# Turning the rows of x with a diagonal of their roots, with g_mix applied per partition

## What is computed

```
y  = x * rsqrt(mean(x * x, axis=-1) + EPS)
xn = y * g_mix
z  = xn @ w_in
```

## Time and profile before

| what | value |
|---|---|
| median of 3 runs | 1081.69 us (1081.29 to 1082.82) |
| the profiled execution's own time | 1082.38 us |
| its span, first to last instruction | 1080.6 us |
| busy over the span | TensorE 90%, weight loads 80%, VectorE 62%, ScalarE 51%, GpSimd 26% |
| bytes moved | 193.67 MB, 179 GB/s over the span |
| chain that ended last, by engine | TensorE 72%, VectorE 14%, issue 7%, ScalarE 4%, DMA 2% |

### The profile page before, as it was taken

One profiled execution on the slowest core, in us unless ns is written; L12 is line 12 of the kernel. 1 busy time (PEld: TensorE's weight loads), 2 busy tenths in 40 slices (PEclk: granted clock), 3 DMA queues, 4 the chain that ended last, 5 costly groups with the idle time before them and its releaser, 6 DMA issues.

```text
span 1080.6 us, 16629 instructions
## 1 busy us (share of the span) xinstructions
PE 975.7 (90%) x5991; PEld 861.5 (80%) x5991; DVE 671.3 (62%) x805; ACT 547.4 (51%) x605; POOL 281.4 (26%) x187
## 2 busy tenths in 40 slices
PE   3989899999999978889999999948899999999960
PEld 2989789888988976789999996837788888888750
DVE  5495659747865972621111211369999898989827
ACT  5544525714542570343333233347787878787722
POOL 2443204313330430433434345000111111101012
PEclk9999999999999998899999999968999999999995
DMA  9352122302222220123232339318999999999835
GB/s 309 125 164 59 47 67 60 94 28 87 62 59 68 58 58 20 40 62 95 79 96 78 97 123 290 149 59 293 399 409 415 413 414 413 414 413 414 314 119 206
DMA packets 146738, 193.67 MB, mean 179 GB/s; under 512 B 14486, under 2 KB 91692, under 8 KB 146576
## 3 DMA queue, kind: packets, MB, share of 16 engines
q1 hardware_dynamic: 139000, 165.27, 43.8%
q0 software_dynamic: 4656, 16.21, 3.9%
q10 hardware_dynamic: 3048, 11.75, 2.8%
HBM read 173.43 MB, written 19.77 MB: 179 GB/s over the span
## 4 chain that ended last, share of the span: by engine, by line
PE 72%; DVE 14%; issue 7%; ACT 4%; DMA 2%; DVEq 1%; POOL 0%; POOLq 0%; ACTq 0%; SPq 0%
PE PJ L447 58%; DVE MEM L1641 2%; DVE MEM_R L1847 2%; PE MS L1293 2%; PE NM L1273 2%; PE PJ L1222 1%; PE MS L1255 1%; PE MS L1456 1%; PE NM L447 1%; PE MS L1300 1%; PE MS L1268 1%; DMA MEM<-in_x_prompt_dram 1%; PE NM L1404 1%; PE MS L1283 1%; DMA MEM<-expert_rows,MEM 1%
## 5 line engine op out<-in xcount | busy, mean ns | idle before, releaser
L447 PE MATMUL PJ<-MEM_R 128*128 128x272 f32 (+2 forms) x5016 | 809.3, 322 | 18.6 <-ACT MEM L857 6.0
L447 PEld LDWEIGHTS PJ<-MEM_R 128*128 128x128 f32 x5016 | 727.8, 192 | 81.3 <-issue 10.3
L661 POOL TENSOR_TENSOR MEM_R<-RAW,MEM_R 128x1024 fp32r<-128x1024 f32 x81 | 201.6, 2498 | 371.1 <-ACT MEM_R L798 371.0
L1847 DVE TENSOR_TENSOR MEM_R<-CHUNK,MEM_R 128x2048 fp32r<-128x2048 f32 x100 | 224.6, 2285 | 16.1 <-ACT MEM_R L1056 14.8
L1056 ACT CAST MEM_R<-CHUNK 128x2048 fp32r<-128x2048 f32 x100 | 189.3, 1912 | 14.3 <-PE PJ L447 10.3
L798 ACT CAST MEM_R<-RAW 128x1024 fp32r<-128x1024 f32 x81 | 84.4, 1051 | 127.8 <-DMA RAW<-in_w_pb_dram 39.2
L1787 DVE TENSOR_TENSOR MERGED<-PJ,MEM 128x544 f32<-128x544 f32 x16 | 11.6, 724 | 148.1 <-PE PJ L447 148.1
L747 POOL COPY MEM<-MEM 128x1 uint32 (+1 forms) x16 | 18.5, 1154 | 237.5 <-PE MS L1456 237.5
L1641 DVE SCALAR_TENSOR_TENSOR MEM<-MEM 128x548 f32<-128x548 f32 x72 | 60.9, 845 | 8.5 <-DVE MEM L1639 0.5
L1065 ACT CAST MEM_R<-MS 128x1024 fp32r<-128x1024 f32 x17 | 17.3, 1016 | 34.9 <-PE MS L1456 34.9
L1255 PE MATMUL MS<-MEM 128*128 128x512 f32 (+4 forms) x80 | 23.3, 436 | 11.6 <-DVE MEM L1681 11.6
(11 more groups left out here) (284 smaller groups left out, 940.3 us busy)
## 6 DMA issues: line engine op xcount, KB each, us to landing
CHUNK<-in_w_gate_dram SPq DMA_DIRECT2D x34, 1024.0 KB, 9.0
CHUNK<-in_w_up_dram SPq DMA_DIRECT2D x34, 1024.0 KB, 10.7
CHUNK<-in_w_down_dram SPq DMA_DIRECT2D x34, 1024.0 KB, 9.3
RAW<-in_w_in_dram SPq DMA_DIRECT2D x56, 512.0 KB, 3.5
expert_rows<-MEM ACTq DMA_DIRECT2D x16, 512.0 KB, 6.0
expert_rows<-MEM SPq DMA_DIRECT2D x8, 512.0 KB, 5.3
RAW<-in_w_pa_dram SPq DMA_DIRECT2D x8, 512.0 KB, 3.7
RAW<-in_w_pb_dram SPq DMA_DIRECT2D x8, 512.0 KB, 3.6
```

What stands on the lines that cost most here:

```text
L447: ins = pe.matmul(out, w(a), x(b), start=first and n == 0, stop=last and n == 2)
L661: tt(lo, raw[slot], hi.bitcast(F32), ALU.subtract).then_inc(lo_done, 1)
L1847: tt(moe_hl[c][1], moe_raw[c], moe_hl[c][0].bitcast(F32), ALU.subtract).then_inc(chunk_lo[c], 1)
```

## The change

Rows of x are no longer rescaled before they are turned. For each row tile VectorE writes a 128 by 128 diagonal matrix of the tile's roots (identity times root), and TensorE multiplies each raw block of x by that diagonal, as an ordinary float32 matmul in place of the transpose: the result is the turned block, scaled by the roots. `g_mix` is loaded as 8 rows of 128 numbers (4 KB in all), turned once by TensorE into 8 columns `gm` with channels on partitions, and applied where the halves are rounded: ScalarE rounds with four activations a half, each with its own column of `gm` as scale per partition, and VectorE forms the rests with four instructions a half (bank times `gm`, minus `xh`). The diagonals of tiles 2, 3 and 4 are written together after the second batch of roots, ahead of the rests of tile 1.

```diff
-        gmb = at("q", D)
+        gm_rows, gm = at("q", P)[0:KT], at("q", KT, plus=P)
+        diag = at("q", J, P, plus=2 * P)
...
-            act.dma_start(gmb, g_mix[0].partition_broadcast(P)).then_inc(gmix_in, 16)
+            act.dma_start(gm_rows, g_mix[0].rearrange("(c p) -> c p", p=P)).then_inc(gmix_in, 16)
...
             act.wait_ge(consts, NCONST)
+            act.wait_ge(gmix_ready, 1)
...
-                    act.copy(xh[:, 4 * half:4 * half + 4, tok(j)], MS[:, half, :].rearrange("p (m n) -> p m n", m=4)[:, :, 0:n])\
-                        .then_inc(xh_ready, 1)
+                    for m in range(4):
+                        kt = 4 * half + m
+                        ins = act.activation(xh[:, kt, tok(j)], MS[:, half, P * m:P * m + n], ACT.Copy, scale=gm[:, kt:kt + 1])
+                    ins.then_inc(xh_ready, 1)
...
+            pe.wait_ge(gmix_in, 16)
+            pe.transpose(NM[:, 0, 0:KT], gm_rows, ident[0:KT, 0:KT]).then_inc(gmix_turned, 1)
+
             for j in range(J):
                 n = rows_of[j]
-                pe.wait_ge(xn_ready, j + 1)
+                pe.wait_ge(diag_ready, j + 1)
...
-                        last = pe.transpose(b[:, P * m:P * m + n], x_in[0:n, j, ds((4 * half + m) * P, P)], ident[0:n, 0:n])
+                        last = pe.matmul(b[:, P * m:P * m + n], x_in[0:n, j, (4 * half + m) * P:(4 * half + m + 1) * P], diag[0:n, j, 0:n],
+                                         start=True, stop=True)
...
-            def normalise(j):
-
-                n = rows_of[j]
-                stt(x_in[0:n, j, :], x_in[0:n, j, :], rstd[0:n, j:j + 1], gmb[0:n], ALU.mult, ALU.mult).then_inc(xn_ready, 1)
+            def root_diagonal(j):
+
+                ts(diag[:, j, :], ident, rstd[:, j:j + 1], None, ALU.mult).then_inc(diag_ready, 1)
...
-                    tt(xl[:, 4 * half:4 * half + 4, tok(j)], x, xh[:, 4 * half:4 * half + 4, tok(j)].bitcast(F32), ALU.subtract)\
-                        .then_inc(x_split, 1)
+                    for m in range(4):
+                        kt = 4 * half + m
+                        ins = stt(xl[:, kt, tok(j)], x[:, m, :], gm[:, kt:kt + 1], xh[:, kt, tok(j)].bitcast(F32), ALU.mult, ALU.subtract)
+                        ins.then_inc(x_split, 1) if m == 3 else st.do(ins)
+                    st.wait()
...
+            dve.wait_ge(gmix_turned, 1)
+            dve.tensor_copy(gm, NM[:, 0, 0:KT]).then_inc(gmix_ready, 1)
             dve.wait_ge(x_root, 1)
             refine(st, slice(0, P), slice(0, 2))
-            dve.wait_ge(gmix_in, 16)
-            normalise(0)
-            normalise(1)
+            root_diagonal(0)
+            root_diagonal(1)
+            dve.wait_ge(gmix_ready, 1)
             rest_of_x(0)
             dve.wait_ge(x_root, 2)
             refine(st, slice(0, P), slice(2, J))
-            normalise(2)
+            root_diagonal(2)
+            root_diagonal(3)
+            root_diagonal(4)
             rest_of_x(1)
-            normalise(3)
             rest_of_x(2)
-            normalise(4)
             rest_of_x(3)
             rest_of_x(4)
```

More of the change, by code:

```diff
@@ L355, in hawk_mlstm_hmoe_kernel @@
         steps_v, steps_a, steps_p = sem("steps_v"), sem("steps_a"), sem("steps_p")
-        x_root, xn_ready, xh_ready, x_split = sem("x_root"), sem("xn_ready"), sem("xh_ready"), sem("x_split")
+        x_root, diag_ready, xh_ready, x_split = sem("x_root"), sem("diag_ready"), sem("xh_ready"), sem("x_split")
         gmix_in, v_turned = sem("gmix_in"), sem("v_turned")
+        gmix_turned, gmix_ready = sem("gmix_turned"), sem("gmix_ready")
         lam_log, f_log, cl_ready = sem("lam_log"), sem("f_log"), sem("cl_ready")
```

## The result

The changed kernel takes 1088.4 us (median of 5 runs) where the kernel before, on the same chip, takes 1082.18: a ratio of 1.0052, 95% interval 1.0035 to 1.0070. It is slower, by about what was forecast. One run in which the chip held a lower clock throughout (1150.66 us) is left out of the ratio and had been the profiled one, so the profile shown here is that of another execution of the same program, which took 1088.26 us.

A forecast was written before the change was run, and what follows sets the result against it. The chain through the first stage was taken to bound the kernel, with bank trips growing to 4.7 us replacing VectorE's 3.85 a tile. Projections near 34.1 against 27.8 worked for before gave +6.3 us, 1088.0 us; range 1082.0 to 1090.1.

The forecast's parts named there:

- the dropped load: Start of the kernel: removing the 0.52 MB g_mix copy was to bring both batches of roots 1.28 us sooner.
- A matmul is two records: Turning on TensorE: a float32 matmul costs two records of 0.243 us, so a half fills in 1.94 instead of 0.97.
- VectorE's half: Subtraction out of a bank: four 128-column instructions with a scalar per partition take 1.13 us a half against 0.69.
- ScalarE's 1.14 against 1.25: Rounding out of a bank: four 128-column activations with a scale per partition were forecast at 1.25 us a half against 0.59.
- The trip through a bank: Turning stage: fill, round, subtract and free in series grow from 2.65 to 4.7 us, above the 3.85 a tile of before.
- fourth rival: Turning: a matmul takes four transpose times, 3.9 us a half, and TensorE is the bound; +20, 1102 us; chance 0.03.
- the overlap of the second: Rival: small instructions overlap like plain ones, 0.75 and 0.82 us a half; +2.7, 1084.4 us; chance 0.11.
- TensorE is at its lower clock here: Turning stage: TensorE taken at 1.2 GHz, six or seven matmuls a us, setting 0.243 us a record.
- first rival: Turning stage: clock rises to 2.4 GHz, trip falls to 3.8 us; +1.9, 1083.6 us; chance 0.18.
- the projections' gain of 1.7 us: First projections: with the clock already up they no longer run 4.3 us at six a us, saving 1.7 us.
- a delay of the first projection is a delay of the whole: Chain after the turning: no link waits on kernel-start timing, so the stage's +6.3 us passes to the total.
- fifth rival: Later chain: the delay is taken up where engines wait for weights; 1081.7 us; chance 0.06.

The follow-up runs named there:

- wide_load_back: Changed kernel with the 0.5 MB copy of g_mix to all partitions loaded again, unused, ahead of the small load: 1088.73 us, ratio 1.0054 against before.
- plain_split: Changed kernel without g_mix: one copy and one subtraction of 512 columns a half, diagonal and matmuls kept: 1080.51 us, ratio 0.9981 against before.
- four_pieces_no_scale: Changed kernel without g_mix: four pieces a half kept on both engines, as plain copies and subtractions: 1084.72 us, ratio 1.0016 against before.
- before_again: Second profile of the unedited kernel before the change: projections start at 27.64 us, experts' loop takes 289.7 us.
- transpose_kept: Changed kernel with plain identity transposes instead of the diagonal matmuls, four pieces kept: 1071.77 us, not comparable (other routing, 16 tiles); projections at 30.22 us.
- after_dense: Changed kernel plus six unused 256-column matmuls, two before each half of the last tile, two before the tables: 1085.08 us, ratio 1.0019 against before.
- g_spread_by_PE: Changed kernel with g_mix loaded as one row, spread by TensorE, multiplied into raw rows; one instruction a half per engine: 1081.87 us, ratio 0.9987 against before.
- g_on_rows: Changed kernel with g_mix loaded to all partitions behind x's first two tiles, multiplied into raw rows; one rounding a half: 1083.65 us, ratio 1.0016 against before.
- run 32: Not a run's label: words from "TensorE had run 32-column matmuls", meaning matmuls of 32 columns in the narrow last tile; no kernel or time belongs to it.

## Why the prediction was right, and where it was not

**The number.** 1088.0 was forecast from 1081.69, +6.3; 1088.4 and 1088.94 were measured against 1082.18 and 1082.52, +6.2 and +6.4. Direction, total and the path that decides held. That the total was met to 0.2 us is luck: it is the sum of a stage 2.9 us better than forecast and of later stretches that are worse.

**What held.** The refining of the first roots starts at 7.19 us, 2.05 sooner than the 9.24 of the earlier trace rows, where 1.28 was taken for the dropped load; wide_load_back prices the load at 1.92. A matmul is two records: sixteen a tile, 3.76 / 16 = 0.235 at the lower clock against 0.243. VectorE's half is 1.13 as worked out from the earlier trace rows; ScalarE's 1.14 against 1.25 from the earlier trace rows. The trip through a bank at the lower clock is 4.57 (18.40 to 22.97) against 4.7. That the bank trip takes the place of VectorE's rescaling as the bound is shown by plain_split, and that the loss lies in the two engines' pieces, in series, by the runs with one of them. The fourfold matmul (fourth rival) is out, and so is the overlap of the second: it holds for the plain pieces alone (0.77 and 0.95 in four_pieces_no_scale, 0.75 and 0.82 forecast), not for the form with an operand.

**The step that failed: "TensorE is at its lower clock here".** It was carried over from the transposes of before to the matmuls. The first half of tile 1 ran at the higher level, the granted clock reads 0.50 from 15.9 to 22.7 us and 1.00 from there to 29.5, and tile 3's eight records took 1.13 us, so its trip is 3.66; the first rival had 3.8 for it. Tile 2, in between, ran low. The first rival was therefore half true, but its second half, the projections' gain of 1.7 us, turned round: the clock fell behind the narrow tile, and the projections ran low for 5.2 us instead of 4.3.

By its own steps: tiles were forecast at 9.5, 14.45, 19.5, 24.2, 28.9 and projections at 34.1; measured 8.72, 14.08, 18.40, 22.97, 26.63 and 31.10. Of the 3.0 us between the two last numbers 0.8 is the earlier start; 0.4 of it is lost again between tiles 0 and 1, where the first rounding stands behind ScalarE's squares; 0.7 and 1.0 come from tiles 1 and 3, in which the clock was up (in tile 1 until 15.9 us), 0.1 from tile 2 and 0.7 from the last.

**The other step: a delay of the first projection is a delay of the whole.** Up to the routing it held. The lateness of the changed kernel's profile against the first profile of before is 3.4 us at the first projection, 3.9 at the gates and at the restart (80.87 against 77.00), 2.6 at the next group of projections (99.52 against 96.91), 4.1 at the routing (735.3 against 731.2) and 5.5 to 5.8 at the end. The dip to 2.6 need not be a gain of the change, nor what follows it a loss. The timeline of the changed kernel in the first head has

```profile
124.34 4.86 PE L1264 MATMUL MS<-MEM 128*128 128x384 f32 x16 [2.27 <-DVE MEM L1694]
```

and the two groups in question, 15.96 and 4.86 us, are near the 15.77 and 4.56 + 0.31 of before_again, where the first profile has 17.22 and 3.34: such figures come without the change too. Against before_again the lateness is 3.5 at the first projection, 3.8 at the gates and at the restart, 4.0 at the next group, 4.1 at the routing and 5.0 to 5.3 at the end. Nothing was absorbed, which rules out the fifth rival. What the forecast did not have is the last 0.9 to 1.7 us, most of it in the experts' loop. There TensorE's clock falls once more; the changed kernel's stretches at its end:

```profile
1025.00:1027.00 2.00, 0.19 (x1) 0.80 0.54 207
1027.00:1029.00 2.00, 2.00 (x5) 0.50 0.94 293
```

Such a fall in the loop is seen in the profiles of four kernels (changed, plain_split, wide_load_back, four_pieces_no_scale), whose loops take 290.8 to 292.5 us, and in the shorter loop of transpose_kept, and not in the others, at 289.5 to 289.7. It is 1.3 us of the changed kernel's 5.8, but plain_split has it too and is the fastest of all with this routing, so it isn't tied to the loss in this stage. Executions of one program differ by as much: of the 88 of the kernel before that were taken beside these experiments, 16 with a mean granted clock of 0.955 took 1083.9 to 1084.7 us, and 42 with 0.958 took 1080.6 to 1083.8. What decides the fall stays open; no run here was made for it.

**So the 6 us, read from the profiles:** 3.4 from the stage, 0.4 from the first projections at the lower clock, 0.4 between the gates and the experts' first product (743.7 against 739.4), 1.3 in the loop and 0.3 behind it, 5.8 of span in all. after_dense shows the clock's part by experiment: although its stage is 1 us longer, it is 1.3 us ahead of the changed kernel at the gates, 2.8 at the routing and 3.9 in the total. Of the rest behind the gates, 1.5 is the first head's group, which differs as much between two profiles of the kernel before, and 1.3 the loop; whether the extra matmuls have a part in these is not shown.

## What to carry to other kernels

Moving a scale from one long instruction with it along the row to several short ones with it per partition costs where those short ones stand in series: price the trip through the bank (fill, round, subtract, free), not the engine that was busiest. A scale along the other axis did best here on the raw rows, beside the trip, from a load too small to hold the first loads back (4 KB in g_spread_by_PE; the 0.52 MB of g_on_rows held x's third tile). And a stage that ends in narrow matmuls with waits between them can hand a low clock to what follows; compare the first 10 us behind a stage, not its end alone.

## What was not expected of the hardware

- Short instructions with an operand per partition were dear. Four pieces of 128 columns out of a bank: on ScalarE 1.14 us with a scale per partition, 0.77 without, 0.59 for one instruction of 512; on VectorE 1.13, 0.95 and 0.69. In the last tile, with 32 columns a piece, the four still take 0.82 to 0.85 us on ScalarE with the scale, 0.46 without and 0.27 as one instruction, and 0.73, 0.48 and 0.29 on VectorE: what is added is added per instruction, hardly per column.
- Float32 matmuls of 128 columns raised the clock within a stage with gaps, where transposes of the same blocks, which keep TensorE busy half as long, ran at five or six a us to the end of the stage. In the changed kernel the clock then fell at 29.5 us, when TensorE had run 32-column matmuls with waits between the halves since 26.63.
- One 0.52 MB load on another queue delayed the squaring of x's first tile by 1.76 us, more than its 1.28 us of bytes at the rate of the earlier trace rows.
